# Adding the residual in the DMAs of GpSimd instead of on VectorE, in the last stage of a hybrid attention layer

## The reference

```python
o = jnp.einsum('bse,ed->bsd', y, w_out[layer])
x = x + rms_norm(o, g_post[layer])
```

## Time and profile before

| | |
|---|---|
| median of the runs | 963.33 us (962.98, 963.68) |
| span of the profiled execution, first to last instruction | 961.3 us |
| TensorE busy | 940.1 us, 98% of the span |
| VectorE, ScalarE, GpSimd busy | 405.0, 312.0, 93.1 us |
| read from HBM, written | 100.29 MB, 5.79 MB |
| mean granted TensorE clock | 0.994 of full speed |

### The profile page before, as it was taken

How to read it: one execution, slowest core, us unless ns; L and a number is a source line. 1 busy time by engine, 2 the same in 40 slices (tenths; PEclk the granted TensorE clock), 3 DMA queues, 4 the chain that set the end, 5 groups by cost and what they waited for, 6 DMA issues and landing times.

```text
span 961.3 us, 12115 instructions
## 1 busy us (share of the span) xinstructions
PE 940.1 (98%) x4556; PEld 790.4 (82%) x4556; DVE 405.0 (42%) x724; ACT 312.0 (32%) x546; POOL 93.1 (10%) x84
## 2 busy tenths in 40 slices
PE   7799999999999999999999999999999999999996
PEld 5798888888888888888888888888888888888885
DVE  5884365444333333334343434343434254241424
ACT  6572333323232222223232323232323243242411
POOL 5542057000000000000010101010101000000000
PEclk9899999999999999999999999999999999999999
DMA  9934333343333333333333333333333127341216
GB/s 309 263 93 125 94 114 85 90 105 93 86 97 87 89 97 87 98 87 99 87 98 88 98 87 98 87 98 87 95 80 95 58 88 289 105 125 50 87 36 227
DMA packets 150943, 104.86 MB, mean 109 GB/s; under 512 B 5561, under 2 KB 136665, under 8 KB 149766
## 3 DMA queue, kind: packets, MB, share of 16 engines
q1 hardware_dynamic: 150630, 103.48, 38.5%
q10 hardware_dynamic: 288, 1.05, 0.3%
HBM read 100.29 MB, written 5.79 MB: 110 GB/s over the span
## 4 chain that ended last, share of the span: by engine, by line
PE 95%; DVE 2%; ACT 1%; DMA 1%; issue 0%; SPq 0%; DVEq 0%; ACTq 0%
PE strip_ps L416 25%; PE strip_ps L418 25%; PE strip_ps L417 25%; PE score_ps L416 3%; PE score_ps L418 3%; PE score_ps L417 3%; PE o_ps L520 3%; PE pt_ps L501 2%; PE score_ps L481 1%; PE score_ps L480 1%; PE score_ps L482 1%; PE o_ps L575 1%; PE vt_ps L464 1%; DMA stage<-in_mem_dram 1%; ACT y L736 1%; DVE y L937 1%
## 5 line engine op out<-in xcount | busy, mean ns | idle before, releaser
L416 PE MATMUL strip_ps<-xT,ring 128*128 128x512 f32 x896 | 352.0, 393 | 0.0
L418 PE MATMUL strip_ps<-xT,ring 128*128 128x512 f32 x896 | 349.3, 390 | 0.0
L417 PE MATMUL strip_ps<-xT,ring 128*128 128x512 f32 x896 | 348.9, 389 | 0.0
L418 PEld LDWEIGHTS strip_ps<-xT,ring 128*128 128x128 f32 x896 | 168.2, 188 | 35.6
L417 PEld LDWEIGHTS strip_ps<-xT,ring 128*128 128x128 f32 x896 | 168.4, 188 | 33.4
L416 PEld LDWEIGHTS strip_ps<-xT,ring 128*128 128x128 f32 x896 | 168.2, 188 | 33.3
L697 ACT ACTIVATE ring<-raw 128x1024 fp32r<-128x1024 f32 x128 | 135.1, 1058 | 34.3 <-PE strip_ps L418 34.3
L937 DVE TENSOR_TENSOR ring<-raw,ring 128x1024 fp32r<-128x1024 f32 x115 | 141.0, 1226 | 6.4 <-ACT ring L697 6.3
L1041 DVE MEMSET pace<- 128x1 f32 x36 | 2.1, 59 | 138.8 <-PE score_ps L482 138.8
L1313 POOL TENSOR_TENSOR bias<-bias,mask 128x128 f32<-128x128 f32 x6 | 6.6, 1097 | 553.0 <-DMA bias<-negc_dram 553.0
L937 DVE TENSOR_TENSOR xT<-raw,xT 128x1024 fp32r<-128x1024 f32 x32 | 39.0, 1224 | 41.9 <-ACT xT L697 41.6
(11 more groups left out here) (164 smaller groups left out, 1021.9 us busy)
## 6 DMA issues: line engine op xcount, KB each, us to landing
raw<-in_w_in_dram SPq DMA_DIRECT2D x112, 512.0 KB, 4.1
raw<-in_w_out_dram SPq DMA_DIRECT2D x32, 512.0 KB, 4.0
raw<-in_w_mem_kv_dram SPq DMA_DIRECT2D x16, 512.0 KB, 6.2
stage<-in_x_dram SPq DMA_DIRECT2D x4, 1024.0 KB, 7.6
xres<-in_x_dram SPq DMA_DIRECT2D x4, 1024.0 KB, 7.5
out_dram<-o_sb SPq DMA_DIRECT2D x16, 256.0 KB, 3.5
toep_dram<-table_dram SPq DMA_DIRECT2D x1, 1536.0 KB
bias<-toep_dram SPq DMA_DIRECT2D x6, 256.0 KB, 2.6
```

What stands on the lines that cost most here:

```text
L416: pe.matmul(dst, lhs[0], rhs[0], start=start, stop=False, skip_group_check=True)
L417: pe.matmul(dst, lhs[1], rhs[0], start=False, stop=False, skip_group_check=True)
L418: return pe.matmul(dst, lhs[0], rhs[1], start=False, stop=stop, skip_group_check=True)
```

## The change

VectorE no longer adds the residual. It scales each tile in two halves of 1024 columns, `tensor_scalar` with the same scale, and counts them with `o_scaled`; it waits for `o_gained` ahead of both halves. GpSimd issues, for each half, one DMA with `accum_op=ALU.add` whose destination is the half of `o_sb` and whose source is the residual: `xres` in SBUF for tiles 0 and 1, `x` in HBM for tiles 2 and 3. Each of the eight has a semaphore of its own, `residual_added`. SyncE waits for it and stores the half, 512 KB. Its two loads of `xres` for tiles 2 and 3 are gone.

```diff
-        final_done = sem("final_done")
+        o_scaled = sem("o_scaled")
+        residual_added = [sem(f"residual_added{i}") for i in range(2 * QB)]
...
             for s in range(QB):
-                for j in range(4):
-                    sp.wait_ge(final_done, 4 * s + j + 1)
-                    sp.dma_start(out[0, P * s:P * (s + 1), S * j:S * (j + 1)],
-                                 o_sb[:, s, S * j:S * (j + 1)]).then_inc(out_stored, 16)
-                if s + 2 < QB:
-                    sp.dma_start(xres[:, s % 2], x[0, P * (s + 2):P * (s + 3), :]).then_inc(xres_landed[s % 2], 16)
-            sp.wait_ge(out_stored, 16 * 4 * QB)
+                for half in range(2):
+                    cols = slice(D // 2 * half, D // 2 * (half + 1))
+                    sp.wait_ge(residual_added[2 * s + half], 16)
+                    sp.dma_start(out[0, P * s:P * (s + 1), cols], o_sb[:, s, cols]).then_inc(out_stored, 16)
+            sp.wait_ge(out_stored, 16 * 2 * QB)
...
                 rstd(TILES + s, s, lambda: gain_out(OCH - 1, s))
-                dve.wait_ge(xres_landed[s % 2], 16 * (s // 2 + 1))
-                for j in range(4):
-                    if j == 3:
-                        dve.wait_ge(o_gained, QB * (OCH - 1) + s + 1)
-                    cols = slice(S * j, S * (j + 1))
-                    dve.scalar_tensor_tensor(out=o_sb[:, s, cols], in0=o_sb[:, s, cols], scalar=stat[:, 4, s:s + 1],
-                                             in1=xres[:, s % 2, cols], op0=ALU.mult, op1=ALU.add
-                                             ).then_inc(final_done, 1)
+                dve.wait_ge(o_gained, QB * (OCH - 1) + s + 1)
+                for half in range(2):
+                    cols = slice(D // 2 * half, D // 2 * (half + 1))
+                    dve.tensor_scalar(o_sb[:, s, cols], o_sb[:, s, cols], stat[:, 4, s:s + 1], None, ALU.mult
+                                      ).then_inc(o_scaled, 1)
...
+            for s in range(QB):
+                for half in range(2):
+                    cols = slice(D // 2 * half, D // 2 * (half + 1))
+                    if s < 2:
+                        pool.wait_ge(xres_landed[s], 16)
+                        source = xres[:, s, cols]
+                    else:
+                        source = x[0, P * s:P * (s + 1), cols]
+                    pool.wait_ge(o_scaled, 2 * s + half + 1)
+                    pool.dma_start(o_sb[:, s, cols], source, accum_op=ALU.add).then_inc(residual_added[2 * s + half], 16)
```

## The result

The changed kernel takes **971.45 us** (971.29 to 971.62, 2 runs) against 963.33: ratio 1.009, 95% interval 1.0074 to 1.0107. It is slower by 0.9%, in the direction forecast, inside the range, and within the 2% band that was given 75%; the forecast was 976.

What follows compares the result with a forecast made beforehand. TensorE bounds the kernel until about 952.7 us, then a serial tail. Transfers from 935.0 run to 962.5; tile 3's accumulate ends at 968.7, its first store 970.2, its last 973.7; plus 2.4 gives 976 us, range 966 to 989.

Steps and rivals of the forecast that it cites:

- 2% band: Times from 944.1 to 982.6 us, which a measurement of this kernel can't tell from no change; given 75%.
- overlap of 0.06 us: On VectorE, one scaling starts some 0.06 us before the previous is reported done, so two take 1.44 us.
- GpSimd's issue: Time GpSimd takes to issue one 512 KB DMA: 1.0 us taken, between 0.33 and 4.4.
- rival in which the issue bounds the tail: Eight GpSimd issues at 4.4 us each from 934.0 end at 969.2, giving 978 us; chance 3%.
- second rule: GpSimd can't write DMA descriptors during VectorE's two-port operations, so tile 3's half 0 is issued 0.7 us later.
- Two passes: Each accumulate reads a second operand, so a tile costs the DMA engines 6.1 us; time 976 us, chance 48%.
- u: DMA time for one pass of a whole 1.05 MB tile: 3.06 us, at 343 GB/s while busy.
- plain-load: Rival: accumulates as quick as plain loads, so tile 3 meets an idle ring; time 967.1 us, chance 20%.
- three-pass rivals: DMA engines read, add and write one after another, 9.2 us per tile or worse; 988 us, chance 25%.
- forecast's formula: With the queue never empty, time is 935.0 + 3(a + u) + a + u/2 + 3.5 + 2.4, a one tile's accumulate.
- last store: Tile 3's final 512 KB store, 3.5 us from issue to landing, at 973.7.
- The queue: DMA transfers of tiles 0 to 2 run through to 962.5, so tile 3, ready at 956.12, finds 5 to 6 us queued.

Runs made afterwards that it cites:

- copy experiment: The changed kernel with GpSimd's eight DMAs copying the residual over the scaled half instead of adding it: 965.82 us, ratio 1.0037 to the kernel before.

## Why the prediction was right, and by how much it missed

- **VectorE.** 1.44 us were forecast for two scalings, 1.42 measured, and the halves of tile 3 came 0.76 and 1.42 us after the chain's last statistic, as said. (The overlap of 0.06 us in the forecast was misread: four of 747 ns in 2.74 us overlap by 0.08, with which the forecast would have been 1.42.) With the DMA engines full from 935 to 967, the gain bought nothing that shows.
- **GpSimd's issue.** 1.0 was taken; it is 0.84 to 1.32 in the changed kernel, and starts about 0.34 us after VectorE is done. The first one of the program starts 1.0 us behind its half; the whole queue waits for that one, and it used up TensorE's earlier end, so that data moves from 935.0 as forecast. The rival in which the issue bounds the tail was wrong: eight issues are 7.4 us of GpSimd's work in 23 us. The second rule, by which half 0 of tile 3 waits for the other half's scaling, didn't show: it was issued at 955.44, before that scaling ended at 955.75.
- **The accumulate, the deciding term.** Two passes, 2u, were taken. The ratio is 1.96 to the stores beside it and 1.85 to GpSimd's own copies, and the copy experiment shows that it is the addition. The rule of the Trainium skill's page "Collectives: The Full Stack", section "The bandwidth ceiling: the fold count and why AG ≠ RS ≠ AR", told there of ReduceScatter between cores, agrees with this trace: 5.55 us against 2.83. The plain-load and the three-pass rivals are out. These runs show the doubled time; that a second read is its reason, as the Trainium skill says, no run here shows.
- **The size of u** was the error. It was read as 3.06 from a stretch of stores in 2 KB rows; 2.83 is what stores in 4 KB rows take beside accumulates, and 2.8 what they take with VectorE's fused form. That is 0.57 less in each of four accumulates and 0.23 in each of 3.5 stores, 3.1 us in all.
- **The rest of the sum.** With the measured 5.55 and 2.83 the forecast's formula gives 935.0 + 22.2 + 9.9 = 967.1 for the moment before the last store, and the last accumulate landed at 966.8, where 970.2 was forecast. The last store, 3.5 forecast and 2.6 measured, is 0.9. The 2.4 us from the last landing to the time were 2.05 (971.45 - 969.4). So 976.1 - 971.45 = 4.65 is 3.1 for u, 0.3 unexplained before the last store, 0.9 for that store and 0.35 at the end.
- **The queue.** Tile 3 was to find 5 to 6 us of queued transfers. With the measured rates the first three tiles keep the engines until 935.0 + 25.1 = 960.1, 4.7 us past tile 3's first issue, so the queue was there and was shorter by what u was too large. Without it the tail is only 3.0 us shorter: the engines then begin 1.6 us after the first issue (957.1, 955.49), a time that the queue had hidden. That this accounts for the whole difference between 4.7 and 3.0 is argued and not measured.
- **Ring space** was no term of the forecast. At 1024 bytes it costs nothing (971.76 with twice as much), and at 512 it would have cost 15 us, a kernel slower by 2.6%. That the kernel had 1024 and not 512 was luck for the forecast, which never asked.

## What to carry to other kernels

Moving an elementwise step from VectorE into a DMA at the end of a kernel saved 1.3 us of VectorE's time per tile here and cost a second transfer in series (3 to 4.5 us, that saving already taken off), an addition at half the DMA rate in the last tile (2 to 3) and a queue (2.4 to 3). Count each added byte twice in the budget of the DMA engines, for the tiles before the last as well, and ask which stores and loads stand behind the accumulates in another engine's queue. An issue of GpSimd's that starts just as an earlier DMA of its lands was here the sign that the ring space was short.

## What the runs showed of the hardware that I had not expected

- With a ring space of 1024 bytes three accumulates of 512 KB are in flight, with 512 bytes one; the second case costs 15 us over eight DMAs.
- GpSimd's issue of a 512 KB copy takes 0.53 to 0.78 us, of an accumulate 0.84 to 1.36.
- On idle engines a store of 512 KB lands 2.6 to 2.7 us after its issue, as does one of 256 KB (2.4 to 2.8).
- An accumulate into HBM takes 6.25 us of DMA time per 1 MB tile, into SBUF 5.55 to 6.0; a copy by GpSimd takes 3.0, a store 2.8 in 4 KB rows and 3.06 in 2 KB rows.
- Open: why, when GpSimd adds into the output, the first issue starts at 936.23 though the first half was scaled by 933.3 and the copies of x into the output had been issued by 797. No run was made for it.
